# Expert stage: running sums gathered, added to and scattered per block, four weight slots, and one row a token at the end

## What is computed

```python
x = x + concat([y_a, y_b]) @ w_out                 # x1, the residual
h2 = rmsnorm(x, norm_ffn)
# top-1 of 4 groups, then top-2 of the 8 experts of that group
for e in range(32):
    he = silu(h2 @ w_gate[e]) * (h2 @ w_up[e])     # 1024 -> 256
    out = out + combine[:, e:e+1] * (he @ w_down[e])
x = x + out
y = rmsnorm(x, norm_final)
```

## Time and profile before

| | us |
|---|---|
| median of three runs | 1045.3 |
| the three runs | 1045.3, 1040.34, 1045.63 |
| the profiled execution, whole | 1041.24 |
| its span in the trace | 1039.5 |
| expert blocks 0 to 31, from the first weight load | 604 to 966 |
| extra pair, to its last scatter landed | 966 to 996.4 |
| final stage | 998.7 to 1039.5 |

### The profile page before, as it was taken

How to read it: one execution, slowest core, us unless ns; L and a number is a source line. 1 busy time by engine, 2 the same in 40 slices (tenths; PEclk the granted TensorE clock), 3 DMA queues, 4 the chain that set the end, 5 groups by cost and what they waited for, 6 DMA issues and landing times.

```text
span 1039.5 us, 15030 instructions
## 1 busy us (share of the span) xinstructions
PE 976.2 (94%) x5448; PEld 829.4 (80%) x5448; DVE 673.7 (65%) x1041; ACT 505.5 (49%) x891; POOL 122.0 (12%) x114
## 2 busy tenths in 40 slices
PE   5999999999999999999999988999999999999855
PEld 4889999999999999998888774677777777777422
DVE  7457776697434535456666575788787878787117
ACT  7487786433233222323222222577666666665215
POOL 2000000000000000000300020243332324222000
PEclk9999999999999999999999998999999999999978
DMA  7114768326754564457222169899998989996557
GB/s 244 42 41 125 168 150 206 109 84 186 204 138 126 163 163 109 141 173 255 77 81 82 45 237 350 311 363 375 361 364 337 355 311 370 336 379 231 184 213 308
DMA packets 118027, 220.89 MB, mean 213 GB/s; under 512 B 68428, under 2 KB 81286, under 8 KB 109262
## 3 DMA queue, kind: packets, MB, share of 16 engines
q1 hardware_dynamic: 105762, 194.20, 56.1%
q0 software_dynamic: 9792, 17.19, 4.6%
q10 hardware_dynamic: 2412, 8.68, 2.1%
HBM read 191.79 MB, written 46.72 MB: 229 GB/s over the span
## 4 chain that ended last, share of the span: by engine, by line
PE 71%; DMA 13%; DVE 9%; ACT 4%; issue 2%; SPq 0%; ACTq 0%; DVEq 0%; POOLq 0%
PE psum L1141 27%; DMA wd<-w_down 11%; PE psum L2044 10%; PE psum L2255 6%; PE psum L2330 4%; PE psum L2259 3%; PE psum L2240 2%; PE psum L1164 1%; PE psum L2296 1%; PE psum L1979 1%; ACT wd_hi L2305 1%; DVE it L953 1%; DVE xi L955 1%; PE psum L2193 1%; PE psum L1246 1%
## 5 line engine op out<-in xcount | busy, mean ns | idle before, releaser
L1141 PE MATMUL psum<-hh,wh 128*128 128x350 f32 x672 | 223.4, 332 | 3.9 <-issue 3.9
L1141 PE MATMUL psum<-hh,wl 128*128 128x350 f32 x672 | 218.0, 324 | 0.0
L1141 PE MATMUL psum<-hl,wh 128*128 128x350 f32 x672 | 217.3, 323 | 0.0
L1141 PEld LDWEIGHTS psum<-hh,wh 128*128 128x128 f32 x672 | 127.8, 190 | 5.3 <-issue 4.1
L1141 PEld LDWEIGHTS psum<-hl,wh 128*128 128x128 f32 x672 | 127.5, 190 | 0.9
L1141 PEld LDWEIGHTS psum<-hh,wl 128*128 128x128 f32 x672 | 127.2, 189 | 0.0
L2231 DVE TENSOR_TENSOR wgu_lo<-wgu,wgu_hi 128x1536 fp32r<-128x1536 f32 x60 | 105.1, 1752 | 6.5 <-ACT wgu_hi L2226 6.2
L2226 ACT ACTIVATE wgu_hi<-wgu 128x1536 fp32r<-128x1536 f32 x60 | 89.0, 1485 | 21.1 <-DMA wgu<-w_up 21.1
L2309 DVE TENSOR_TENSOR wd_lo<-wd,wd_hi 128x2048 fp32r<-128x2048 f32 x30 | 68.8, 2292 | 38.8 <-ACT wd_hi L2305 38.6
L2255 PE MATMUL psum<-wgu_hi,xgt_hi 128*128 128x512 f32 x180 | 85.5, 475 | 0.0
L2184 POOL DMA_INDIRECT expert_rows<-out,slot_rows x34 | 54.2, 1593 | 253.2 <-DVE out L2348 245.7
(11 more groups left out here) (350 smaller groups left out, 1832.7 us busy)
## 6 DMA issues: line engine op xcount, KB each, us to landing
wgu<-w_gate SPq DMA_DIRECT2D x34, 1024.0 KB, 7.2
wgu<-w_up SPq DMA_DIRECT2D x34, 1024.0 KB, 15.4
wd<-w_down SPq DMA_DIRECT2D x34, 1024.0 KB, 16.2
wst<-w_in SPq DMA_DIRECT2D x28, 512.0 KB, 3.9
ck<-qkv_rows SPq DMA_DIRECT2D x9, 702.0 KB
qkv_rows<-acc SPq DMA_DIRECT2D x12, 520.0 KB, 6.1
xb<-x SPq DMA_DIRECT2D x8, 512.0 KB, 4.2
wo<-w_out SPq DMA_DIRECT2D x8, 512.0 KB, 6.9
```

The source lines that it names most:

```text
L1141: ins = mm(ps[:, c, 0:ZC], w[:, kk, :], a[:, kk, c * ZC:(c + 1) * ZC], start=(kk == 0 and q == 0), stop=(kk == KD - 1 and q == 2))
```

## The change

The tensor `expert_rows` (two rows a token) goes, and `sum_rows` (`b.sum_d`, one row a token) takes its place. While the output projection runs, the residual `x1` is stored there, nine tiles (`residual_stored`). Each block then gathers the running sums of its tokens into `before` (`gather_sum`), one DVE instruction multiplies the down product by the weight and adds the gathered sums into `total` (`add_rows`, in the place of `weigh_a` on ACT and `weigh_b` on DVE), and POOL scatters `total` back (`scatter_sum`). So that a sum isn't read before it is written, consecutive blocks are of different groups (`expert_of`), and POOL waits for the scatter of block e-2 before it gathers the sums of block e+2.

There are four weight slots and four `xg` buffers. Step j of `staggered` is now: `front` of j+2, `half` of j, `early` of j+2 (first half of gate and up, high and low), `mid` of j+1, `late` of j+2 (second half), `back` of j. The loop has four steps an iteration in the place of six. The first extra pair is in this pipeline, behind conditionals, with the same matmuls in parts; the sums of block 32 are gathered only when all 32 blocks before are scattered, and those of block 33 only when block 32 is scattered. The final stage loads one row a token on SP, takes the norm and stores on SP; the additions, PE's part and ACT's DMAs are gone. Other parts of the diff, left out below, drop the second row index from the routing tables and rename semaphores.

```diff
...
-    b.ye = nc.dram_tensor("expert_rows", (2 * TOK, D), F32, kind="Internal").ap()
+    b.sum_d = nc.dram_tensor("sum_rows", (TOK, D), F32, kind="Internal").ap()
...
+    def residual_stored(eng, t):
+        n = rows(t)
+        eng.dma_start(b.sum_d[t * P:t * P + n, :], b.x1[0:n, t, :]).then_inc(b.x1_out.sem, 16)
...
+                residual_stored(sp, t - 2)
...
+        sp.wait_ge(x1_ok, T - 1)
+        residual_stored(sp, T - 2)
...
-        load_gate_up(sp, b, io, 1, 1)
+        load_gate_up(sp, b, io, expert_of(0), 0)
+        load_down(sp, b, io, expert_of(0), 0)
+        load_gate_up(sp, b, io, expert_of(1), 1)
...
-        load_down(sp, b, io, 1, 1)
+        load_down(sp, b, io, expert_of(1), 1)
+        sp.wait_ge(b.x1_out.sem, b.x1_out.at(16 * T))
+        load_gate_up(sp, b, io, expert_of(2), 2)
+        load_down(sp, b, io, expert_of(2), 2)
         sample.wait_added(sp)
         sample.store(sp)
-        load_gate_up(sp, b, io, 2, 2)
-        load_down(sp, b, io, 2, 2)
+        load_gate_up(sp, b, io, expert_of(3), 3)
+        load_down(sp, b, io, expert_of(3), 3)
...
+        pool.wait_ge(iota, 4)
         h2_stored(pool)
         pool.wait_ge(b.rows_ok, 1)
-        for k in range(SLOTS):
-            gather(pool, b, k, k)
+        for k in range(3):
+            gather(pool, b, k, expert_of(k))
+        pool.wait_ge(b.x1_out.sem, b.x1_out.at(16 * T))
+        gather(pool, b, 3, expert_of(3))
...
-    for k, at in enumerate((b.D, b.D + 24576, b.L)):
+    for k, at in enumerate((b.D, b.D + 24576, b.R1 + 4096, b.L)):
...
-SLOTS = 3
+SLOTS = 4
...
+def expert_of(block):
+    return EPG * (block % GRP) + block // GRP
...
+    def gather_sum(pool, q, p, e):
+        pool.indirect_dma_start(before[p][:, :], None, b.sum_d, rows_of(e), bounds_check=TOK - 1, oob_is_err=False
+                                ).then_inc(q.sum_in.sem, 16)
+    def scatter_sum(pool, q, p, n, e):
+        pool.wait_ge(q.sum_ok.sem, q.sum_ok.at(n + 1))
+        pool.indirect_dma_start(b.sum_d, rows_of(e), total[p][:, :], None, bounds_check=TOK - 1, oob_is_err=False
+                                ).then_inc(q.sum_out.sem, 16)
...
-    def weigh_a(act, q, p, n, e):
-        act.wait_ge(q.down_ok.sem, q.down_ok.at(n + 1))
+    def add_rows(dve, q, p, n, e):
+        dve.wait_ge(q.down_ok.sem, q.down_ok.at(n + 1))
+        dve.wait_ge(q.sum_in.sem, q.sum_in.at(16 * (n + 1)))
...
-            act.wait_ge(q.scattered.sem, q.scattered.at(16 * n))
-        nc.scalar.activation(out[p][:, 0:512], ps[0:C, 4 + 2 * p, :], ACT.Copy, scale=weight(e)
-                             ).then_inc(q.outa_ok.sem, 1)
-    def weigh_b(dve, q, p, n, e):
-        dve.wait_ge(q.down_ok.sem, q.down_ok.at(n + 1))
-        if later(n):
-            dve.wait_ge(q.scattered.sem, q.scattered.at(16 * n))
-        nc.vector.tensor_scalar(out[p][:, 512:D], ps[0:C, 5 + 2 * p, :], weight(e), None, ALU.mult
-                                ).then_inc(q.outb_ok.sem, 1)
+            dve.wait_ge(q.sum_out.sem, q.sum_out.at(16 * n))
+        nc.vector.scalar_tensor_tensor(
+            total[p][:, :].rearrange("c (h d) -> c h d", h=2), ps[0:C, 4 + 2 * p:6 + 2 * p, :], weight(e),
+            before[p][:, :].rearrange("c (h d) -> c h d", h=2), ALU.mult, ALU.add).then_inc(q.sum_ok.sem, 1)
...
+    def staggered(eng, front, half, early, mid, late, back):
         def step(j, i=0):
-            if j + 2 < NE:
-                front(block_of(j + 2, i))
+            front(block_of(j + 2, i))
             half(block_of(j, i))
-            if j + 1 < NE:
-                mid(block_of(j + 1, i), block_of(j + 2, i) if j + 2 < NE else None)
-            back(block_of(j, i), block_of(j + 2, i) if j + 2 < NE else None)
+            early(block_of(j + 2, i))
+            mid(block_of(j + 1, i))
+            late(block_of(j + 2, i))
+            back(block_of(j, i))
...
-        with loop(0, 4) as i:
-            for j in range(2, 8):
+        with eng.Fori(1, 7) as i:
+            for j in range(4):
                 step(j, i)
...
+        for e in range(28, NE - 2):
+            step(e)
+        eng.wait_ge(b.ove_ok.sem, b.ove_ok.at(1))
+        eng.wait_ge(b.extra_ok.sem, b.extra_ok.at(1))
+        count = extra_blocks(eng)
...
+        with if_extra():
+            front(first)
+        half(block_of(NE - 2))
+        with if_extra():
+            early(first)
+        mid(block_of(NE - 1))
+        with if_extra():
+            late(first)
+        back(block_of(NE - 2))
+        with if_extra():
+            front(second)
+        half(block_of(NE - 1))
+        with if_extra():
+            early(second)
+            mid(first)
+            late(second)
+        back(block_of(NE - 1))
+        with if_extra():
+            half(first)
+            mid(second)
+            back(first)
+            half(second)
+            back(second)
...
-                x = block_of(j, i)
+                x, y = block_of(j, i), block_of(j + SLOTS, i)
                 sp.wait_ge(x.q.gu_ok.sem, x.q.gu_ok.at(x.n + 1))
-                load_gate_up(sp, b, io, x.e + SLOTS, x.k)
+                load_gate_up(sp, b, io, y.id, x.k)
...
+            with sp.If_lt(sp.to_reg(0), count):
+                for p in range(2):
+                    x = block_of(NE + p - SLOTS)
+                    e = extra_expert(0, p)
+                    sp.wait_ge(x.q.gu_ok.sem, x.q.gu_ok.at(x.n + 1))
+                    load_gate_up(sp, b, io, e, x.k)
+                    sp.wait_ge(x.q.down_ok.sem, x.q.down_ok.at(x.n + 1))
+                    load_down(sp, b, io, e, x.k)
...
             final.loads(sp)
+            final.stores(sp)
...
+            for p in range(2):
+                gather_sum(pool, main[p], p, expert_of(p))
+            pool.wait_ge(main[0].turned.sem, main[0].turned.at(1))
+            gather(pool, b, 0, expert_of(SLOTS))
+            for e in range(NE):
+                x, y = block_of(e), block_of(e + 1)
+                if e == NE - 5:
                     pool.wait_ge(b.ove_ok.sem, b.ove_ok.at(1))
                     pool.wait_ge(b.extra_ok.sem, b.extra_ok.at(1))
...
-                if e < NE - 1:
-                    x = block_of(e)
-                    pool.wait_ge(x.q.turned.sem, x.q.turned.at(x.n + 1))
-                    if e + SLOTS < NE:
-                        gather(pool, b, x.k, e + SLOTS)
...
-                            gather(pool, b, x.k, e + SLOTS, more_gathered[e + SLOTS - NE].sem)
-                if e >= 1:
-                    x = block_of(e - 1)
-                    scatter(pool, x.q, x.p, x.n, e - 1)
...
+                if e + 5 < NE:
+                    pool.wait_ge(y.q.turned.sem, y.q.turned.at(y.n + 1))
+                    gather(pool, b, y.k, expert_of(e + 5))
+                elif e + 5 < NE + 2:
+                    with pool.If_lt(pool.to_reg(0), count):
+                        pool.wait_ge(y.q.turned.sem, y.q.turned.at(y.n + 1))
+                        gather(pool, b, y.k, e + 5)
+                pool.wait_ge(x.q.sum_ok.sem, x.q.sum_ok.at(x.n + 1))
+                if e + 2 < NE:
+                    if x.n > 0:
+                        pool.wait_ge(x.q.sum_out.sem, x.q.sum_out.at(16 * x.n))
+                    gather_sum(pool, x.q, x.p, expert_of(e + 2))
+                scatter_sum(pool, x.q, x.p, x.n, expert_of(e))
+            with pool.If_lt(pool.to_reg(0), count):
+                for p in range(2):
+                    pool.wait_ge(main[p].sum_out.sem, main[p].sum_out.at(16 * (NE // 2)))
+                for p in range(2):
+                    x = block_of(NE + p)
+                    gather_sum(pool, x.q, p, x.id)
+                    scatter_sum(pool, x.q, p, x.n, x.id)
+                    pool.wait_ge(x.q.sum_out.sem, x.q.sum_out.at(16 * STEPS))
...
-    def second_loads(act):
+            sp.dma_start(y[t][0:n, :], b.sum_d[t * P:t * P + n, :]).then_inc(e_in[t].sem, 16)
+    def stores(sp):
         for t in range(TILES):
             n = rows(t)
-            act.dma_start(y1[t][0:n, :], b.ye[TOK + t * P:TOK + t * P + n, :]).then_inc(e_in[t].sem, 16)
+            sp.wait_ge(o_ok.sem, o_ok.at(t + 1))
+            sp.dma_start(io.y[t * P:t * P + n, :], y[t][0:n, :]).then_inc(left.sem, 16)
+        sp.wait_ge(left.sem, left.at(16 * TILES))
...
-            if t in SUMMED:
-                act.wait_ge(summed.sem, summed.at(SUMMED.index(t) + 1))
-                nc.scalar.activation(y0[t][0:n, :].rearrange("p (c n) -> p c n", c=2), in_psum(t), ACT.Square,
-                                     accum_out=b.stat[0:n, t, 0:1]).then_inc(sq.sem, 1)
-            else:
-                act.wait_ge(x2_ok.sem, x2_ok.at(added.index(t) + 1))
-                nc.scalar.activation(y0[t][0:n, :], b.x1[0:n, t, :], ACT.Square, accum_out=b.stat[0:n, t, 0:1]
-                                     ).then_inc(sq.sem, 1)
+            act.wait_ge(e_in[t].sem, e_in[t].at(16))
```

(63 more changed lines are left out.)

356 lines of the change are left out of this document (127 added, 229 removed).

## The result

The changed kernel takes 1050.4 us (median of 6 runs, 1048.3 to 1053.3) against 1043.3 for the kernel before on the same chip: a ratio of 1.008, with a 95% interval from 1.0055 to 1.0096. The forecast was 1027 and the range ended at 1047. The kernel is slower by 0.8%, where I had given 78% to faster.

The account below looks back on a forecast made before the run. The DMAs were to bound the loop at 10.4 us a block: weights in at 964, final loads at 996.7, plus 24.5 and 1.74 gave 1023 us against the profiled 1041.24, or 1027 on the median; range 1008 to 1047.

Parts of the forecast that it names:

- So the DMAs become the bound of the loop, at 10.4 us: Block loop: the added gather of sums lifts DMA work from 9.69 to 10.40 us a block, above PE's 9.74.
- so I expect the DMA share near 1: Block loop: the fourth weight slot adds one block time to a load's 15 us, so the DMAs stay nearly full.
- L: The moment when the last gate and up weights (block 33) are in, after the loop's loads; forecast at 964 us.
- the share of 0.91 in the earlier trace: DMA share from 760 to 920 us in the kernel before, read as the DMAs not being full.
- the wait of 16.39 us: Loop of the kernel before: a wait on a down weight, too long for the some 15 us three slots leave.
- The early 0.98: DMA share from 690 to 760 us in the kernel before, where PE and the DMAs were both read as full.
- rival B: Loop: the fourth slot doesn't raise the DMA share from 0.91; 11.4 us a block, 1055 us; chance 0.13.
- C, the sums' landing: Loop: with three indirect DMAs on q0, gathered sums land after over 16 us; at 18 us, 1057 us; chance 0.07.
- D, the conditionals: After the loop: conditionals at the end cost 7.5 to 10 us, making 1036 us; chance 0.12.
- A: Loop: PE sets the pace at 9.74 us a block, giving 1012 to 1015 us with short gathers; chance 0.20.
- The edits called hidden: Loop: changed DVE, ACT and POOL work and the wait for gathered sums fit under 10.4 us a block, costing nothing.
- The final stage and the chain ahead of it: After L: 32.7 us of serial gathers, additions and scatters to the final loads, then 24.5 us against 40.8.

## Why the prediction was wrong

- **The failed step: "So the DMAs become the bound of the loop, at 10.4 us" and "so I expect the DMA share near 1".** 10.40 us was the mean of 16 engines, 9.69 before plus 0.71. The added gather puts 7.7 of its rows on the fullest engine, .159 x 7.7 = 1.22 us and not 0.71, on a base of 9.93 (changed kernel without the sums' rows) and not 9.69. Its work is 11.15 us a block, and 11.35 was measured. With the rows so placed the share stood at 0.92 and 0.95, and the loop waited for the DMAs all the same. The extra 0.95 us over 27 or 28 blocks is 26 us, and L was 25.8 us late.
- **The reading under it.** I took the share of 0.91 in the earlier trace rows as idle time of which more slots would win back 9%, and the wait of 16.39 us as a stop of PE for a load that started too late. That piece runs from the load's issue to its landing; PE itself stood idle for only 6.0 of the 160 us. Three slots against four moved the pace by nothing (11.34 and 11.35). The kernel before was held by its fullest engine too, 10.20 us for 9.88 of work: spreading its tokens alone takes 12 us off.
- **The early 0.98, which I held against rival B,** came, as I now read it, while weights loaded ahead were still being used up, as did the 1.00 from 640 to 690 us in the changed kernel. No run tests this.
- **Rival B** has the right numbers (a share of 0.91, 11.4 us a block, L = 992, 1055 us) and the wrong mechanism. It has loads that are issued too late; here each is issued 30 us before it lands, nearly three blocks, so that others always stand in the queue, and issuing them a block later left the pace at 11.34 us. I gave it 0.13.
- **C, the sums' landing,** did not come true, as forecast. Gathers of sums land in 7.8 to 9.2 us from 690 to 960 us, and from 640 us to the end of the blocks DVE waits for one once, 4.6 us, at block 32. **D, the conditionals:** 33.7 us from L to the loads against 32.7 leaves no room for its 7.5 to 10 us, but doesn't price them, since the terms of that chain missed both ways (last item). **A** (PE sets the pace, 1012 to 1015 us) is what the changed kernel does once it is spread: 9.76 us a block and 1010.4 us.
- **The edits called hidden** were: with the sums' rows left out and every instruction kept, PE is busy 160 of 160 us.
- **The final stage and the chain ahead of it** were right to 1.1 and 1.0 us, the chain partly by luck. By POOL's rows above, two scatters took 5.9 and 3.8 us from their start to the next gather's, where I had 2.6, and two gathers 5.3 and 5.4 us to the next scatter's start, where I had 6.7 (4.5, 1.3 and 0.9): 4.6 us too little and 2.7 too much, and the 1.0 is what is left after smaller ones. Why the first of these scatters took so long, no run shows. The shorter end is what the change gains: with the tokens spread in both, it takes 1031.4 to 1010.4 us, 21 us less. As it was run, the loop gave all of it back.

So the sum with one term put right, 11.15 + 0.2 for 10.40 (the 0.2 is fitted, being the 11.35 measured less the 11.15 worked out), gives L = 990, 1023 + 26 = 1049 us against the profiled execution and 1027 + 26 = 1053 on the median.

## What to carry to other kernels

A mean DMA share of 0.9 with a queue that always holds transfers need not be headroom: look for a single full engine behind it, and sum the work of each engine by the partitions it serves. Where the DMAs set the pace, an indirect DMA that skips out-of-range rows should have its valid rows dealt over all sixteen groups of eight partitions. That costs other numbers in one constant table and was worth 40 us in the changed kernel and 12 in the kernel before; the rebuilt expert stage itself is worth 21. A landing time that follows the number of slots shows how early a load was issued; only the pace shows what the DMAs need.
